# One core, two transformer blocks in float32: w_out with its tokens as rows, the gate broadcasts between w_a and w_out, h2 evicted by two engines, the router's exponential ahead of the h2 copies

## What is computed

```python
ya = ya @ w_a + b_a
m = jax.nn.sigmoid(g_a) * ya + jax.nn.sigmoid(g_b) * yb
y = m @ w_out + b_out
x = _layer_norm(DEEPNORM_ALPHA * x + g1 * y, post1_g, post1_b)
h = _layer_norm(x) * (1 + sc2) + sh2
logits = (xt @ w_router + b_router).astype(jnp.float32)   # xt: h, 256 x 1024; 32 experts
top_logits, top_idx = lax.top_k(logits, TOP_K)            # 4
top_w = jax.nn.softmax(top_logits, axis=-1)
# each expert on its tokens: act(xb @ w_gu[e] + b_gu[e]) @ w_dn[e] + b_dn[e], weighed by top_w
x = _layer_norm(DEEPNORM_ALPHA * x + g2 * y, post2_g, post2_b)
```

## Time and profile before

| | |
|---|---|
| time, median of 3 runs | 2313.61 us (2311.02 to 2316.53) |
| profiled execution: its own time | 2318.56 us |
| profiled execution: span | 2316.8 us |
| TensorE busy | 2059.3 us, 89% |
| VectorE, ScalarE, GpSimd busy | 856.3, 388.4 and 61.7 us |
| DMA, mean | 250 GB/s |

### The profile page before, as it was taken

How to read it: one execution, slowest core, us unless ns; L and a number is a source line. 1 busy time by engine, 2 the same in 40 slices (tenths; PEclk the granted TensorE clock), 3 DMA queues, 4 the chain that set the end, 5 groups by cost and what they waited for, 6 DMA issues and landing times. The chain is left out here.

```text
span 2316.8 us, 27597 instructions
## 1 busy us (share of the span) xinstructions
PE 2059.3 (89%) x10805; PEld 1299.8 (56%) x10805; DVE 856.3 (37%) x1408; ACT 388.4 (17%) x467; POOL 61.7 (3%) x126
## 2 busy tenths in 40 slices
PE   5999995998989899989899898699988876769997
PEld 3758784333333333333333333489868765657986
DVE  1296335111111111111111112555557664544654
ACT  1011101000000000000000001145334421113541
POOL 2000002000000000000000000100000000000000
PEclk9999897999999999999999999799999886979999
DMA  9478333959999998999998957445554200124552
GB/s 361 163 277 285 122 113 128 386 238 411 421 420 420 420 421 351 393 420 420 420 420 334 387 222 290 141 131 186 194 163 146 91 1 1 55 69 135 183 200 73
DMA packets 142660, 579.94 MB, mean 250 GB/s; under 512 B 10521, under 2 KB 12041, under 8 KB 93259
## 3 DMA queue, kind: packets, MB, share of 16 engines
q1 hardware_dynamic: 135824, 563.12, 62.6%
q0 software_dynamic: 3552, 12.61, 1.7%
q10 hardware_dynamic: 3131, 1.98, 0.3%
HBM read 576.62 MB, written 1.05 MB: 249 GB/s over the span
## 5 line engine op out<-in xcount | busy, mean ns | idle before, releaser
L1000 PE MATMUL bank<-ring,area 128*64 128x512 f32 x1632 | 370.5, 609 | 0.7 <-issue 0.5
L224 DVE TENSOR_TENSOR ring_r<-ring,ring_r 128x2048 fp32r<-128x2048 f32 x92 | 210.8, 2292 | 209.4 <-ACT ring_r L221 208.6
L1000 PEld LDWEIGHTS bank<-ring,area 128*64 128x64 f32 x1632 | 124.4, 141 | 232.8 <-issue 229.4
L722 PE MATMUL bank<-area,ring 128*128 128x256 f32 x1024 | 232.1, 390 | 10.1 <-issue 8.2
L722 PEld LDWEIGHTS bank<-area,ring 128*128 128x128 f32 x1024 | 200.3, 196 | 43.2 <-issue 12.2
L1895 DVE TENSOR_SCALAR area<-bank 128x512 f32<-128x512 f32 x36 | 24.9, 691 | 524.2 <-PE bank L1000 524.2
L221 ACT ACTIVATE ring_r<-ring 128x2048 fp32r<-128x2048 f32 x92 | 175.8, 1912 | 234.4 <-PE bank L759 209.5
L756 PE MATMUL bank<-area_r,ring_r 128*128 128x256 f32 x704 | 200.7, 285 | 2.2 <-DVE area_r L1787 2.2
L758 PE MATMUL bank<-area_r,ring_r 128*128 128x256 f32 x704 | 199.4, 283 | 0.0
L759 PE MATMUL bank<-area_r,ring_r 128*128 128x256 f32 x704 | 199.3, 283 | 0.0
L1038 PE MATMUL bank<-ring,area 128*64 128x512 f32 x848 | 188.6, 595 | 0.5 <-DVE area L1909 0.5
(11 more groups left out here) (295 smaller groups left out, 2126.8 us busy)
## 6 DMA issues: line engine op xcount, KB each, us to landing
ring<-in_w_gu SPq DMA_DIRECT2D x182, 1024.0 KB, 14.2
ring<-in_w_dn SPq DMA_DIRECT2D x94, 1024.0 KB, 14.6
area<-in_w_gu SPq DMA_DIRECT2D x74, 1024.0 KB, 12.9
ring<-in_mlp_w SPq DMA_DIRECT2D x64, 1024.0 KB, 5.4
area<-in_w_dn SPq DMA_DIRECT2D x34, 1024.0 KB, 16.6
ring<-in_w_mod SPq DMA_DIRECT2D x24, 1024.0 KB, 7.9
ring<-in_w_in SPq DMA_DIRECT2D x24, 1024.0 KB, 9.0
ring<-in_gdn_w_in SPq DMA_DIRECT2D x16, 1024.0 KB, 5.5
```

Of the source, the lines that this page charges most:

```text
L224: nc.vector.tensor_tensor(unit_low(i), raw, unit_high(i), ALU.subtract).then_inc(w_split, 1)
L722: ins = mm(bank(g)[:, m * S:(m + 1) * S], u[k // UK][:, k % UK, c:c + P], xT[:, k, :], start=k == 0, stop=k == ND - 1)
L1000: ins = mm(bk[hf * BLK:(hf + 1) * BLK, :], x[:, kt, :], block_u[:, c:c + BANK], start=False, stop=kt == ND - 1)
```

## The change

1. w_out is computed token-major. y is evicted as `bank * g1_bc` into a(7) and added to x_tok, with statistics after each piece; `y_tok` and its transpositions are gone. b_out comes by a broadcast DMA from GpSimd's queue, is multiplied with g1, and goes into x_tok with the factor ALPHA1 ahead of w_out's results.
2. g1 and g2 are both spread by 16 matmuls (`gates_bc`) between w_a and w_out; the diagonals are made after `mix`, and ACT copies the four banks out. `g2_bc` with its eight matmuls after h2_tok is gone.
3. h2T is evicted by ACT (groups 0 and 2) and DVE (groups 1 and 3), and the router starts with the first group. DVE clears two small tiles in place of two areas of 2048 columns.
4. ACT loads the exponential's table with a dummy activation and takes the exponential before the h2_tok copies.
5. The first expert's token count is read before the first gather (PE) and before gateT (DVE). Gather banks and one condition of SP's queue follow the new groups.

```diff
@@ -245,8 +245,8 @@
-                ("w_b", 4), ("yaT", 4), ("w_a", 4), ("w_out", 4), ("y_tok", 4), ("h2T", 4),
-                ("router", 1), ("h2_tok", 4), ("g2_bc", 2), ("pos", 1), ("gateT", 1)):
+                ("w_b", 4), ("yaT", 4), ("w_a", 4), ("gates_bc", 4), ("w_out", 4), ("h2T", 4),
+                ("router", 1), ("h2_tok", 4), ("pos", 1), ("gateT", 1)):
...
@@ -416,7 +418,8 @@
-g2_diag = half(8, 0)
+gate_diag = apad[:, :, :].rearrange("p m t -> p (m t)")[:, 0:2 * D].rearrange("p (h d) -> p h d", d=P)
+g1_bc, b_out_bc = a(8)[:, 0:D], a(8)[:, D:2 * D]
...
@@ -472,11 +475,13 @@
-def experts(eng, steps, overflow, last_block):
+def token_count(eng, e):
+    return eng.value_load(counts[0:1, e:e + 1], min_val=0, max_val=S)
+def experts(eng, steps, overflow, last_block, first_count):
-        n_tok = eng.value_load(counts[0:1, e:e + 1], min_val=0, max_val=S)
+        n_tok = first_count if e == 0 else token_count(eng, e)
...
@@ -524,7 +530,7 @@
-                full(sp, G("g2_bc", 1))
+                emptied(sp, G("w_out", 3))
...
@@ -623,12 +629,16 @@
+    for q in range(4):
+        emptied(pool, G("yaT", q))
+    pool.dma_start(b_out_bc, A["b_out"][0:1, :].to_broadcast([P, D])).then_inc(b_out_in, 16)
+    full(pool, G("gates_bc", 3))
...
@@ -918,32 +928,30 @@
+    pe.wait_ge(diag_ready, 1)
+    for q in range(4):
+        g = G("gates_bc", q)
+        claim(pe, g)
+        for i in range(4):
+            ins = mm(bank(g)[:, i * P:(i + 1) * P], ones[:, :], gate_diag[:, 4 * q + i, :],
+                     start=True, stop=True)
+            settle(ins)
+        fills(ins, g)
-    feature_major("w_out", "w_out", feat(6), C)
-    to_tokens("y_tok", feat(7), wait=lambda hf: (emptied(pe, G("w_out", 2 * hf)),
-                                                 emptied(pe, G("w_out", 2 * hf + 1))))
+    token_major("w_out", "w_out", tokens_of(feat(6)), C)
-    for q in range(4):
-        emptied(pe, G("h2T", q))
+            if t == 0 and k % 2 == 0:
+                emptied(pe, G("h2T", k // 2))
-    pe.wait_ge(diag_ready, 1)
-    for q in range(2):
-        g = G("g2_bc", q)
-        claim(pe, g)
-        for i in range(4):
-            ins = mm(bank(g)[:, i * P:(i + 1) * P], ones[:, :], g2_diag[:, 4 * q + i, :],
-                     start=True, stop=True)
-        fills(ins, g)
...
@@ -1057,12 +1065,10 @@
-    assert all(G("g2_bc", q) % BANKS not in (4, 6) for q in range(2)) and G("gateT") % BANKS not in (4, 6)
+    first_count = token_count(pe, 0)
-        gather_pair((bX, bU)[dh], 0, dh)
+        gather_pair(banks[FIRST[dh]], 0, dh)
-    for q in range(2):
-        emptied(pe, G("g2_bc", q))
...
@@ -1397,20 +1403,30 @@
+    for q in range(4):
+        g = G("gates_bc", q)
+        full(act, g)
+        if q < 2:
+            for i in range(4):
+                emptied(act, G("yaT", i))
+            empties(f(g1_bc[:, q * BANK:(q + 1) * BANK], bank(g)[:, :], ACT.Copy), g)
+        else:
+            empties(f(g2_bc[:, (q - 2) * BANK:(q - 1) * BANK], bank(g)[:, :], ACT.Copy), g)
-                                 scale=sc2p[:, m:m + 1]))
+                                 scale=sc2p[:, m:m + 1]), (0, 2))
+    f(cond[:, 0, 0:1], minus_half[:, 0:1], ACT.Exp)
+    act.wait_ge(route_ready, 1)
+    for t in range(NT):
+        ins = f(R["ex"][:, t, :], R["tmp"][:, t, :], ACT.Exp)
+    ins.then_inc(moe_act, 1)
-    act.wait_ge(route_ready, 1)
-    for t in range(NT):
-        ins = f(R["ex"][:, t, :], R["tmp"][:, t, :], ACT.Exp)
-    ins.then_inc(moe_act, 1)
...
@@ -1725,6 +1742,13 @@
+    for m in range(2 * ND):
+        c = 16 + m if m < ND else 32 + m
+        n[0] += 1
+        v.tensor_scalar(gate_diag[:, m, :], ident[:, :], modc[:, c:c + 1], None, ALU.mult)\
+            .then_inc(dve_step, 1)
+    dve.wait_ge(dve_step, n[0])
+    tick(diag_ready)
...
@@ -1764,17 +1788,15 @@
-    dve.wait_ge(m_ready, 4)
-    for q in range(4):
-        g = G("w_out", q)
-        full(dve, g)
-        for m in range(2):
-            mi = 2 * q + m
-            ins = v.tensor_scalar(feat(7)[:, mi, :], bank(g)[:, m * S:(m + 1) * S], col("b_out", mi),
-                                  modc[:, 16 + mi:17 + mi], ALU.add, ALU.mult)
-            if m == 0:
-                link(ins)
-        empties(ins, g)
+    dve.wait_ge(b_out_in, 16)
+    for q in range(2):
+        emptied(dve, G("gates_bc", q))
+    link(v.tensor_tensor(b_out_bc, b_out_bc, g1_bc, ALU.mult))
+    for t in range(NT):
+        n[0] += 1
+        v.scalar_tensor_tensor(x_tok[:, t, :], x_tok[:, t, :], ALPHA1, b_out_bc, ALU.mult, ALU.add)\
+            .then_inc(dve_step, 1)
+    dve.wait_ge(dve_step, n[0])
...
@@ -1807,18 +1829,31 @@
-    residual("y_tok", ALPHA1)
+    gated_y = a(7)
+    for hf in range(NH):
+        cs = slice(hf * BANK, (hf + 1) * BANK)
+        for t in range(NT):
+            i = NT * hf + t
+            g, y = G("w_out", i), gated_y[:, i * BANK:(i + 1) * BANK]
+            full(dve, g)
+            empties(v.tensor_tensor(y, bank(g)[:, :], g1_bc[:, cs], ALU.mult), g)
+            emptied(dve, g)
+            link(v.tensor_tensor(x_tok[:, t, cs], x_tok[:, t, cs], y, ALU.add))
+            piece_stats(x_tok, t, hf)
-    for m in range(ND):
-        n[0] += 1
-        v.tensor_scalar(g2_diag[:, m, :], ident[:, :], modc[:, 40 + m:41 + m], None, ALU.mult)\
-            .then_inc(dve_step, 1)
-    dve.wait_ge(dve_step, n[0])
-    tick(diag_ready)
-    link(v.memset(w6[:, :], 0.0))
-    link(v.memset(w7[:, :], 0.0))
+    for q in (1, 3):
+        g = G("h2T", q)
+        full(dve, g)
+        for m in range(2):
+            mi = 2 * q + m
+            ins = v.tensor_scalar(feat(1)[:, mi, :], bank(g)[:, m * S:(m + 1) * S], sc2p[:, mi:mi + 1],
+                                  modc[:, 24 + mi:25 + mi], ALU.mult, ALU.add)
+            if m == 0:
+                link(ins)
+        empties(ins, g)
+    link(v.memset(y_blk, 0.0))
+    link(v.memset(spread_T, 0.0))
...
@@ -1917,19 +1952,16 @@
+    first_count = token_count(dve, 0)
-    for q in range(2):
-        g = G("g2_bc", q)
-        full(dve, g)
-        empties(v.tensor_copy(g2_bc[:, q * BANK:(q + 1) * BANK], bank(g)[:, :]), g)
-                           banks[(4, 6)[dh]][:, :].rearrange("p (d s) -> p d s", s=2 * BLK)))
+                           banks[FIRST[dh]][:, :].rearrange("p (d s) -> p d s", s=2 * BLK)))
```

10 lines of the change are left out of this document (7 added, 3 removed).

## The result

The changed kernel took **2327.24 us** (median of 20 runs, 2319.56 to 2336.32), the kernel before beside it 2318.32 (20 runs, 2309.36 to 2331.16). The ratio is **1.0034, with a 95% interval of 1.0020 to 1.0048**. Measured again it was 1.0028 (1.0010 to 1.0047). The kernel before, run unchanged as if it were a change, gave 1.0023 (1.0008 to 1.0038); so the intervals are somewhat too narrow here, and the loss lies between nothing and 0.5%. A gain it is not. The forecast of 2305.8 us, with a range up to 2312.5, is wrong.

The account below looks back on a forecast made before the run. TensorE, busy 2059.3 of 2316.8 us, was taken as the bound, so its standstills ahead of the experts counted. Terms -9.3 in front and +1.5 in the experts gave -7.8: 2305.8 us, range 2301.6 to 2309.6, to 2312.5 with one more long wait.

Parts of the forecast that it names:

- Slower: Rival, experts' branches: long waits widen to experts 3, 7, 11 and so on; from three on +9.3, 2322.9 us; chance 0.07.
- Gates and w_out: From w_a's end to w_out's end: 16 gate matmuls fill idle time, token-major w_out 28.5 us; +0.5, bounds 0 and +3.7.
- w_out's tail: From w_out's last matmul to the last statistics: three DVE operations, 2.1 us, for 6.33; -4.2, bounds -3.9 and -4.5.
- h2T: From h2T's first transposition to the router's start: some 3.8 us for 6.62; -2.8, bounds -1.9 and -3.0.
- The router's clock: Router, 6.32 us before: more of it at the upper clock without the 2.95 us gap; -1.7, bounds 0 and -2.8.
- Router to gather: From the router to the first gather: 7.7 us for 8.85; -1.1, bounds 0 and -2.2.
- Gather to expert 0: From the first gather to expert 0: order and work stay; 0, bounds -1.7 and +3 for the clock.
- Front: All terms ahead of the experts together: -9.3 us.
- The experts: PE's branch waits before experts: long waits move by two experts, still six, nine middle waits for eight; +1.5, bounds -6, +15.
- the first rival: One long wait more, before expert 6 or 3: +5.4 on the forecast, 2311.2 us, within 0.2% of before; chance 0.16.
- Behind the experts: Stages after the experts, such as pooling and delta rule: the prediction's sum has no term for them.
- chance of faster: Whole kernel: a measured time below 2309.0 us, given 0.67, beside same 0.26 and slower 0.07.

## Why the prediction was wrong

**The step that failed** is in the first paragraph: "Nothing else of size runs then, so each microsecond taken out here moves all that follows". It moves, but not unchanged. Some stages behind have a length that depends on when they come: pool_tok, put at nothing, took 24.0 us in place of 13.6. I had read the clock's column as far as the first expert, and taken for the 1900 us behind it that they are the same code. The row 1467.00 to 1480.60 would have shown a stage full of matmuls right behind a stretch at the lower clock, 3.7 us after its return. That is a length of 13.6 us that can become 24, and it should have been a bound of +10 in the sum, and a rival on the other side. No rival of mine had this mechanism; the one called *Slower* asked for three more long waits, and there was one.

By its own steps, from the first pair of traces where nothing else is said:

- **Gates and w_out**, +0.5: 31.0 us from w_a's end to w_out's, for 31.47; -0.4, just below the bound of 0. The gates took 3.7 us as forecast and w_out 27.6 for 28.5, the groups of 7.13 being some 0.2 us too long each. But the 31.47 wasn't typical: w_out took 29.58 us in three of six traces of the kernel before and 27.89 in three. Against their mean it is +0.4.
- **w_out's tail**, -4.2: -4.1. Right.
- **h2T**, -2.8: -2.9. Right, and undone it comes back whole in the trace.
- **The router's clock**, -1.7: -2.2 in this trace, but +0.7, outside the bounds, in the five of twelve in which it took 7.0 us; over six traces of each kernel -1.2. The term was a mean over two outcomes and stood as one.
- **Router to gather**, -1.1: -1.2. Right, and the exponential's order is worth 1.5 us of this stretch.
- **Gather to expert 0**, 0 with bounds -1.7 and +3: +2.1. The clock was 0.77 for 0.95. Mis-sized, inside its bound.
- Front: -9.3 forecast. The steps above come to -8.7 in the first pair; w_a itself was 1.4 us shorter, without cause in the change. Over six traces of each kernel (both plain ones, and those with added matmuls or multiplications behind the experts), from w_a's start to expert 0, the means are 111.2 and 104.3 us: **-6.9**. The router's clock, -1.2 for -1.7, and the way from gather to expert 0, +2.0 for 0, make up the difference.
- **The experts**, +1.5: the idle time grew by 1.6, and expert 6 joined the long waits. But the first pair flatters it. From expert 0 to expert 31 the same six traces have 1010.0 to 1016.6 us, mean 1013.1, and 1015.6 to 1025.0, mean 1019.8: **+6.7**. PE's idle time in front of experts is 56.7 us in the mean before and 61.1 now, +4.4, and its busy time between them 945.2 and 948.1, +2.9, for the same instructions; that this is the clock behind the waits is a reading. One long wait more at the price that the prediction gave it (5.4) and the +1.5 of the rest come to 6.9, so the first rival had this term right, and I had given it 0.16. In the traces this term eats the front's gain, which fits that the two kernels are equal once the clock is held up. The padding of 135 instructions took back some 3 of the 6.7 by one trace; what the rest is, is open.
- **Behind the experts**, 0 without a word: +10.4 in the pooling, and 6 us in the delta rule in three of eleven traces of the changed kernel and its variants.

-6.9 + 6.7 + 10.4 is +10, and the medians say +8.4 to +8.9. The difference may be that not each run of the kernel before holds the clock in the pooling, and not each run of the changed one loses it; the traces, one for each set of runs, can't show it.

One sum of the prediction doesn't come out: its chance of faster, 0.67, is 0.63 by the terms it names (nine tenths of 0.62, a quarter of 0.16, and 0.03).

Not tried: w_out with tokens as rows alone, and the gate broadcasts alone. Their terms rest on the rows above.

## What to carry to other kernels

- Before a saving in front is passed on to the end, look through the clock's column behind it for stages that run at the upper clock close behind a stretch at the lower. Their length is a bound of the sum, and a change of 0.3% is smaller than one of them.
- When a change loses and its own stretch is faster, compare the two traces stage by stage for the first place where the distance shrinks. Then move that stage by a microsecond or two in **both** kernels. If the same delay makes one faster and the other slower, it is the moment.
- Idle time just ahead of such a stage is the cheapest place for matmuls of no use: in the changed kernel 42 of them gave 7 us and 77 more in the delta rule 9, 0.7% in all for no change of the algorithm; the kernel before gained 0.4% by both. And what follows a branch that waits is on the path, even where it is hidden otherwise.

## What the runs showed of the hardware

- **A full TensorE can lose the upper clock and stay at the lower.** pool_tok kept PE busy for 24.04 of 24.04 us; the clock was at 1.00 for the first 1.41 us and at 0.50 for the other 22.63. The stage has one matmul of one row for each two of 128. The same instructions held the upper clock for all 13.6 us when they came sooner behind its return, and with added matmuls ahead of them. The delta rule's last stage took 36.17 us at 0.54 in one trace and 28.14 at 0.81 in another; PE was busy for 24.95 and 16.92 us of it.
- **When the clock changes isn't bound to the instructions.** Of the same code, it came back 3.3 to 5.7 us behind the pooling's first matmul. The Trainium skill (TensorE: Matmul & The Clock Gate, What's actually happening) says that the gate doesn't start afresh with a kernel, so that the number of slow matmuls at its start differs from run to run, and that this is under 1% of a typical span and that their count is not to be fitted. The pooling lies in the middle of a kernel, but the traces agree as to the variation, 3.3 to 5.7 us, and to the size: 10 us are 0.4%. But the outcome differed by kernel, not only by run, 13.6 us in both plain traces of before and 24 in both of the changed kernel, and 0.4% was more than the change was worth.
- **Long waits of branches go by place in the program, not by the length of the branch.** 67 instructions ahead moved the long waits by one expert, 135 by two; a branch over 100 instructions waited 5.66 us right behind one that had passed over 200 in 0.33.
- **The spread.** Twenty runs of one kernel lie within 22 us of each other (2309.4 to 2331.2 for the kernel before), and its six traces (with added work behind the experts in four) differ by 4.2 us up to w_a, by 3.5 from there to expert 0, and by 6.6 in the experts. With 20 runs of each kernel the interval reached 3.2 us to either side, with 12 against 23 or more 3.5 to 5.8, with 6 some 7. A forecast of 8 us can be told from nothing by the first two, a term of 3 us by none. And the kernel before, against itself, came out 0.23% apart.
